# The pooling stage of an odd mixer, interleaved with the gate half of the projection before it

## The chip, the core and the metric

The kernel runs on one core of a Trainium2 chip. The metric is the time of one execution in microseconds (us); a run's time is a little more than the span between its first and last profiled instruction.

## The reference

The program computes two two-layer blocks over 256 tokens of width 2048. The change touches the odd layer of the second block, which is the last layer of the program. In short:

```python
h = u @ w_in_o                                  # 2048 -> 4096
xp, gate = split(h, 2)                          # 2048 columns each
for g, w in enumerate((2, 4, 8, 16)):           # groups of 512 columns
    z[g] = window_mean(xp[g], w, axis=rows) - xp[g]      # over a 4 x 64 grid of tokens
    z[g] = z[g] @ w_pool[g]                     # 512 x 512
y = (concat(z) * pool_scale * silu(gate)) @ w_out_o      # 2048 -> 2048
x = layer_norm(alpha * x + gt * y) * ln_g + ln_b
```

`gt` is a row computed from the conditioning vector (adaptive modulation); the modulation also scales and shifts `x` into `u`.

## The kernel before

**Weights come as a stream.** Every weight is a sequence of slots of 128 x 1024 f32 (512 KB): one slot holds two blocks of 128 rows by 512 columns. The SyncE queue loads slot n into `stage` (a ring of 4, `RING`) as soon as slot n-4 has been split. ScalarE (ACT) writes the high half `wh` (`split_hi`, L257), VectorE (DVE) the rest `wl` (`split_lo`, L278); both are rings of 4 (`SPLITS`), so `split_hi` of slot n waits until TensorE (PE) is done with slot n-4. For a slot PE does 12 matmuls of 128x512 (two row blocks, two token tiles, three products: L325 to L327) and counts it in `split_free`. Eight slots make a group of 512 output columns, accumulated in one of two PSUM tiles `L[0]`, `L[1]`; a group may begin when the group two before it has been evacuated (`psum_free`).

**The stationary operand** is the transposed activation, `xth` and `xtl` (high part and rest). PE transposes two tiles of 128 columns for both token tiles (4 transposes, L404) into one of two PSUM banks `TP`; ACT copies to `xth` (`turn_plain`, L424), DVE subtracts to `xtl` (L430) and frees the bank. The m-th such turn serves the m-th slot of a group.

**The order of the odd layer.** All engines run programs in a fixed order and meet at semaphores:

1. Projection, 8 groups (`R_ODD0`): the first four give `Z` (the pooled half, arena columns 0 to 4095), the last four `gate` (4096 to 8191). ACT evacuates each by Copy (L784). The first group also holds the turns of its input. DVE does one multiply-add of the next modulation (`mod_some`, L569) after every second split. On PE the first two groups are written out and groups 2 to 7 are a loop of three passes, `pe.Fori`, over two groups each.
2. After the last group ACT applies Silu to the whole gate (L1004), and PE computes the sums over tokens, one group of 512 columns after another: 4 plain f32 matmuls (8 passes in the trace, L1975) into the two banks `AB`; DVE scales by the counts and subtracts (L1516), and counts `pooled`. The sums of group g wait for `pooled` of group g-1, since they use the same banks.
3. The pooled `Z` is turned, and the pool product (`R_POOL0`, 8 slots, two for each group) runs between the turns. DVE evacuates group g (`evac_pool`): times `pool_scale` out of PSUM (L1525), then times the gate (L1528).
4. When the last group is through (`y_done`), PE turns the result for the output product (`R_OUTO0`, 4 groups) and ACT issues three loads of 1 MB each, `row_load` (L958): the bias row of the modulation over the gate's columns, `ln_g` and `ln_b` over the windows, the pool scale and what lies beside them. After the first of these groups PE broadcasts the modulation (`modulation_gate`, L1781, 8 passes) and DVE adds the bias row (`gate_rows`, L1456). DVE evacuates each group into the residual. Layer norm and the store of the output follow.

Of the kernel before, what the change touches and what calls it, by code (L numbers as in the profile page):

```python
# [19 lines left out]
P = 128  # L20
# [94 lines left out]
def build(nc, A, out):  # L115
    ctx = ExitStack()
    with ctx:
# [482 lines left out]
        def _(act):  # L600
# [386 lines left out]

            def turn_y(m):
                turn_plain(m)
                if m == 4:  # L990
                    act.wait_ge(once("y_done"), 1)
                    row_load(0, "ln_g", 12288)
# [8 lines left out]
            split_pairs(act, split_hi, R_ODD0, 2, evac_to(0, 1024, 2048), turn=lambda m: turn_modulated(m, 2))  # L1001
            split_pairs(act, split_hi, R_ODD0 + 4, 2, evac_to(4096, 1024, 2048))
            act.wait_ge(psum_free, G_BLOCK1 + R_KV + R_EVEN + R_OUT + R_ODD + 2)
            nc.scalar.activation(ar(4096, 4096), ar(4096, 4096), ACT.Silu).then_inc(once("gate_silu"), 1)  # L1004
            turn_and_split(act, split_hi, R_POOL0, turn_plain)
            act.wait_ge(once("y_done"), 2)
# [3 lines left out]
            split_pairs(act, split_hi, R_OUTO0, R_OUT // 2, None, final=True, turn=turn_plain)  # L1010
# [4 lines left out]
        def _(dve):  # L1015
# [493 lines left out]
            split_pairs(dve, split_lo, R_ODD0, 2, None, turn=turn_x1, beside=lambda i, n: mod_some(64 + 8 * i, n))  # L1509
            split_pairs(dve, split_lo, R_ODD0 + 4, 2, None, beside=lambda i, n: mod_some(80 + 8 * i, n))  # L1510
            Z, gate = ar(0, TT, D), ar(4096, TT, D)
            for g in range(4):
# [7 lines left out]
            def evac_pool(g):  # L1520

                dve.wait_ge(split_free, SPLITS + 8 * R_POOL0 + 2 * g + 2)
                cs = slice(COLS * g, COLS * g + COLS)
                for t in range(TT):
                    ins = nc.vector.tensor_tensor(Z[:, t, cs], L[g % 2][:, t, :], ar(10240 + COLS * g, COLS), ALU.mult)  # L1525
                ins.then_inc(psum_free, 1)
                dve.wait_ge(psum_free, G_BLOCK1 + R_KV + R_EVEN + R_OUT + R_ODD + g + 3)
                ins = nc.vector.tensor_tensor(Z[:, :, cs], Z[:, :, cs], gate[:, :, cs], ALU.mult)  # L1528
                if g == 3:
                    ins.then_inc(once("y_done"), 1)  # L1530

            def turn_z(m):
                turn_plain(m)
                if m == 2:
                    dve.wait_ge(once("pool_row"), 16)
                    dve.wait_ge(once("gate_silu"), 3)
                if m >= 5 and m % 2:
                    evac_pool((m - 5) // 2)

# [3 lines left out]
            def turn_y1(m):  # L1543
                turn_plain(m)
                if m == SLOTS + 1:
                    gate_rows(1)
# [554 lines left out]
```

## Time and profile before

| quantity | value |
|---|---|
| median of three runs | 1954.29 us (1950.17, 1954.29, 1955.58) |
| the profiled execution's own time | 1952.87 us |
| its span, first to last instruction | 1951.0 us |
| PE busy | 1770.0 us, 91% |
| DVE busy | 1331.8 us, 68% |
| ACT busy | 939.3 us, 48% |
| mean granted TensorE clock | 0.957 of full |

Times inside the profile are counted from the span's start. PE is the engine's matmuls, PEld its loads of stationary operands, which overlap them. A matmul's recorded duration overlaps its neighbours', so rates are read from starts, from counts over a stretch, or from the chain, which gives each instruction only the time until the next.

### The profile page before, as it was taken

To read this page: it belongs to the slowest core of one execution; us is meant where nothing else is said; L and a number is where in the kernel's file an instruction comes from. 1 tells how busy PE (TensorE), PEld (TensorE's weight loads), DVE (VectorE), ACT (ScalarE), POOL (GpSimd) and SP (SyncE) were. 2 spreads that over 40 slices of the span, in tenths; PEclk is the share of its full clock that TensorE was granted. 3 is DMA by queue.
4 is the path that set the end of the run, shared out by engine and by line. 5 is a ranking of instruction groups with operands and counts; after the bars stand their busy time and mean duration, and the time that the engine had idled before them with its cause. 6 is when DMAs were issued, how large, how long until landed. Compare 5 with 4: busy or idle time off the path is not lost.

```text
span 1951.0 us, 22381 instructions
## 1 busy us (share of the span) xinstructions
PE 1770.0 (91%) x8116; PEld 1417.6 (73%) x8116; DVE 1331.8 (68%) x1777; ACT 939.3 (48%) x1389; POOL 139.2 (7%) x197
## 2 busy tenths in 40 slices
PE   6998999979998999789999999989998959998894
PEld 5877777868876777568757877777777848885673
DVE  4966777878675777767736677777775556664654
ACT  5445563435365643444464455555533374443334
POOL 0100000111100000111101100000100001110000
PEclk9999999989999999889989999999998979999997
DMA  8855444678654545969936843333846548882551
GB/s 270 288 180 175 150 159 157 206 263 282 225 172 130 176 145 186 317 219 361 315 103 221 281 153 118 113 103 103 316 156 237 192 139 281 289 291 101 186 180 66
DMA packets 107011, 390.30 MB, mean 200 GB/s; under 512 B 12407, under 2 KB 13183, under 8 KB 105215
## 3 DMA queue, kind: packets, MB, share of 16 engines
q1 hardware_dynamic: 75040, 268.99, 39.7%
q0 software_dynamic: 27648, 100.68, 16.8%
q10 hardware_dynamic: 4224, 19.31, 2.6%
q8 instruction: 62, 1.02, 0.2%
q14 instruction: 37, 0.30, 0.0%
HBM read 384.74 MB, written 4.19 MB: 199 GB/s over the span
## 4 chain that ended last, share of the span: by engine, by line
PE 73%; DVE 14%; ACT 5%; DMA 4%; issue 4%; ACTq 0%; SPq 0%; DVEq 0%
PE L L325 20%; PE L L327 19%; PE L L326 19%; DMA mstage<-in_w_mod 3%; PE TP L404 3%; DVE wl L278 3%; DVE macc L569 2%; PE AB L1642 1%; DMA stage<-in_w_stream 1%; PE AB L1571 1%; ACT wh L257 1%; PE AB L1647 1%; PE AB L1975 1%; PE TP L1656 1%; PE AB L1646 1%
## 5 line engine op out<-in xcount | busy, mean ns | idle before, releaser
L278 DVE TENSOR_TENSOR wl<-stage,wh 128x1024 fp32r<-128x1024 f32 x504 | 613.4, 1220 | 321.0 <-ACT wh L257 320.4
L325 PE MATMUL L<-wh,xth 128*128 128x512 f32 x1952 | 797.3, 408 | 7.6 <-DVE wl L278 5.9
L257 ACT ACTIVATE wh<-stage 128x1024 fp32r<-128x1024 f32 x504 | 530.6, 1056 | 498.6 <-PE L L327 417.1
L327 PE MATMUL L<-wh,xtl 128*128 128x512 f32 x1952 | 770.6, 395 | 0.0
L326 PE MATMUL L<-wl,xth 128*128 128x512 f32 x1952 | 769.6, 394 | 0.0
L325 PEld LDWEIGHTS L<-wh,xth 128*128 128x128 f32 x1952 | 373.3, 191 | 101.5 <-issue 19.2
L327 PEld LDWEIGHTS L<-wh,xtl 128*128 128x128 f32 x1952 | 371.6, 190 | 81.4
L326 PEld LDWEIGHTS L<-wl,xth 128*128 128x128 f32 x1952 | 372.6, 191 | 75.4 <-issue 3.4
L569 DVE SCALAR_TENSOR_TENSOR macc<-mstage,scols,macc 128x1024 f32<-128x1024 f32 x240 | 306.7, 1278 | 19.5 <-DMA mstage<-in_w_mod 18.8
L593 POOL DMA_DIRECT2D mstage<-in_w_mod x192 | 138.8, 723 | 1613.2 <-DVE macc L569 1252.2
L879 ACT ACTIVATE arena<-arena 128x256 f32<-128x256 f32 (+1 forms) x136 | 48.2, 426 | 63.6 <-DVE arena L1390 63.5
L1097 DVE SCALAR_TENSOR_TENSOR pa<-tab,AB 128x384 f32<-128x384 f32 x48 | 26.6, 553 | 73.4 <-PE AB L1642 43.4
L679 ACT ACTIVATE pa<-TP 128x384 f32<-128x384 f32 x48 | 23.6, 491 | 108.0 <-PE TP L1656 108.0
L404 PE MATMUL TP<-ident,arena 128*128 128x128 f32 x344 | 55.1, 295 | 22.0 <-DVE xtl L430 7.6
L667 ACT ACTIVATE pa<-pa,st 128x128 f32<-128x128 f32 x96 | 43.0, 448 | 59.8 <-DVE st L1106 36.3
L404 PEld LDWEIGHTS TP<-ident,arena 128*128 128x128 f32 x344 | 44.3, 153 | 33.3 <-issue 9.1
L1571 PE MATMUL AB<-ones,macc 128*128 128x1 f32 x192 | 27.7, 277 | 38.2 <-DVE macc L569 38.2
L404 PE MATMUL TP<-ident,X 128*128 128x128 f32 x144 | 24.5, 302 | 39.5 <-DVE X L1491 19.2
L1571 PEld LDWEIGHTS AB<-ones,macc 128*128 128x128 f32 x192 | 27.9, 231 | 39.8 <-DVE macc L569 39.5
L404 PEld LDWEIGHTS TP<-ident,X 128*128 128x128 f32 x144 | 19.8, 157 | 44.0 <-issue 21.2
L424 ACT ACTIVATE xth<-TP 128x512 fp32r<-128x512 f32 x40 | 23.4, 590 | 52.3 <-PE TP L404 52.3
L643 ACT ACTIVATE arena<-L,st 128x512 f32<-128x512 f32 x60 | 37.8, 682 | 16.8 <-PE L L327 15.4
(184 smaller groups left out, 1391.2 us busy)
## 6 DMA issues: line engine op xcount, KB each, us to landing
stage<-in_w_stream SPq DMA_DIRECT2D x504, 512.0 KB, 4.4
mstage<-in_w_mod POOLq DMA_DIRECT2D x192, 512.0 KB, 6.2
X<-in_x SPq DMA_DIRECT2D x4, 512.0 KB, 8.7
arena<-in_ctx ACTq DMA_DIRECT2D x1, 2048.0 KB, 13.7
x_kept<-X ACTq DMA_DIRECT2D x1, 2048.0 KB, 9.8
X<-x_kept ACTq DMA_DIRECT2D x1, 2048.0 KB, 8.5
arena<-in_b_ada ACTq DMA_DIRECT2D x2, 1024.0 KB, 8.7
arena<-in_ln_b ACTq DMA_DIRECT2D x2, 1024.0 KB, 12.1
```

The costliest lines, as they stand in the source:

```text
L257: nc.scalar.activation(wh[:, s % SPLITS].rearrange("p a b -> p (a b)"), stage[:, s % RING, :], ACT.Copy).then_inc(hi_ready, 1)
L278: nc.vector.tensor_tensor(wl[:, s % SPLITS].rearrange("p a b -> p (a b)"), stage[:, s % RING, :], wh[:, s % SPLITS].rearrange("p a b -> p ...
L325: nc.tensor.matmul(o, xh, w[0], start=start, stop=False, skip_group_check=True)
L326: nc.tensor.matmul(o, xh, w[1], start=False, stop=False, skip_group_check=True)
L327: last = nc.tensor.matmul(o, xl, w[0], start=False, stop=True, skip_group_check=True)
L404: last = nc.tensor.transpose(bank[0:width, j, t * P:t * P + P], src(t), ident[:])
L569: nc.vector.scalar_tensor_tensor(out=acc, in0=block, scalar=col, in1=acc, op0=ALU.mult, op1=ALU.add).then_inc(mod_sum, 1)
L593: pool.dma_start(mstage[:, unit % MOD_UNITS, :].rearrange("p (c n) -> p c n", c=2), WM[n // KPB, :, 2 * cp:2 * cp + 2, COLS * k:COLS * k + ...
L643: ins = nc.scalar.activation(dst(t), L[bank][:, t, :], fn, scale=scale(t))
L667: ins = nc.scalar.activation(pr[b][:, a:a + w], pr[b][:, a:a + w], ACT.Exp, bias=ngm[:, 2 * b + t:2 * b + t + 1], scale=1.0 if swa else ML ...
L879: return nc.scalar.activation(dst, src, ACT.Exp, scale=1.0 / 16)
L1571: last = nc.tensor.matmul(AB[1][:, 384 + 8 * w + j:385 + 8 * w + j], macc[:, w, P * j:P * j + P], ones[:, 0:1], start=True, stop=True)
```

## The change

The odd layer's steps 1 to 4 are put in another order on ACT, DVE and PE; the arithmetic is the same but for the Silu, which now reads the gate's groups from PSUM. The loads on the SyncE and GpSimd queues are as before. The last seven groups of the projection are written out on PE, with no loop.

- The sums of groups 0 to 3 go between slots of the gate groups: after slots 33, 41, 49 and 53 of the projection's 64 (counted from 0). DVE does its part (`pooled`) after its split of slots 38, 46, 54 and 58.
- ACT evacuates the gate groups with Silu (eight pieces of 128x512) in place of Copy and the one large Silu.
- The eight turns of the pooled `Z` follow the eight slots of the last gate group, one each.
- The pool product's eight slots run without those turns. The turns of the result go in pairs (`turn_y`): after pool slots 3, 5 and 7, and before the third slot of the output product. Each pair waits for one group's `y_done` in place of one wait for all.
- `row_load` waits for the fourth `y_done` and comes behind the eighth turn on ACT. `gate_rows` stands after the split of the 11th slot of the output product (the 12th is split after the first residual group).

```diff
+            Z, gate = ar(0, TT, D), ar(4096, TT, D)
             act.wait_ge(mod_cols, MOD_COLS)
             act.dma_start(ar(8192, 3, 512), A["windows"]).then_inc(once("windows"), 16)
             act.dma_start(ar(10240, D), A["pool_scale"][0, :].partition_broadcast(P)).then_inc(once("pool_row"), 16)
-            split_pairs(act, split_hi, R_ODD0, 2, evac_to(0, 1024, 2048), turn=lambda m: turn_modulated(m, 2))
-            split_pairs(act, split_hi, R_ODD0 + 4, 2, evac_to(4096, 1024, 2048))
-            act.wait_ge(psum_free, G_BLOCK1 + R_KV + R_EVEN + R_OUT + R_ODD + 2)
-            nc.scalar.activation(ar(4096, 4096), ar(4096, 4096), ACT.Silu).then_inc(once("gate_silu"), 1)
-            turn_and_split(act, split_hi, R_POOL0, turn_plain)
-            act.wait_ge(once("y_done"), 2)
+            hi.n = 8 * R_ODD0 + 4
+            ODD, POOL, OUTO = 8 * R_ODD0, 8 * R_POOL0, 8 * R_OUTO0
+            for m in range(2):
+                turn_modulated(m, 2)
+            for n in range(4, 68):
+                if n < 10:
+                    turn_modulated(n - 2, 2)
+                hi()
+                if n >= 60:
+                    turn_plain(n - 60)
+                if n % 8 == 3 and n > 8:
+                    g = (n - 11) // 8
+                    slots_done(act, ODD + n - 3)
+                    for t in range(TT):
+                        dst = (Z if g < 4 else gate)[:, t, COLS * (g % 4):COLS * (g % 4) + COLS]
+                        ins = nc.scalar.activation(dst, L[g % 2][:, t, :], ACT.Copy if g < 4 else ACT.Silu)
+                    ins.then_inc(psum_free, 1)
+            hi(4)
+            for i in range(4):
+                if i:
+                    hi(2)
+                for m in range(2 * i, 2 * i + 2):
+                    turn_plain(m)
+            act.wait_ge(once("y_done"), 5)
             row_load(1, "b_ada", 4096)
             row_load(1, "ln_g", 12288)
             row_load(1, "ln_b", 8192)
-            split_pairs(act, split_hi, R_OUTO0, R_OUT // 2, None, final=True, turn=turn_plain)
+            hi(OUTO + 4 * SLOTS - hi.n)
             layer_norm_act(1, 2 * DEPTH + 3)
...
-            split_pairs(dve, split_lo, R_ODD0, 2, None, turn=turn_x1, beside=lambda i, n: mod_some(64 + 8 * i, n))
-            split_pairs(dve, split_lo, R_ODD0 + 4, 2, None, beside=lambda i, n: mod_some(80 + 8 * i, n))
+            lo.n = 8 * R_ODD0 + 4
             Z, gate = ar(0, TT, D), ar(4096, TT, D)
-            for g in range(4):
+            GO = G_BLOCK1 + R_KV + R_EVEN + R_OUT
+            def pooled(g):
                 dve.wait_ge(once("pool_sums"), g + 1)
                 for t in range(TT):
                     z = Z[:, t, COLS * g:COLS * g + COLS]
...
             def evac_pool(g):
-                dve.wait_ge(split_free, SPLITS + 8 * R_POOL0 + 2 * g + 2)
+                slots_done(dve, 8 * R_POOL0 + 2 * g + 2)
                 cs = slice(COLS * g, COLS * g + COLS)
+                if g == 0:
+                    dve.wait_ge(once("pool_row"), 16)
+                    dve.wait_ge(psum_free, GO + R_ODD + 2)
                 for t in range(TT):
                     ins = nc.vector.tensor_tensor(Z[:, t, cs], L[g % 2][:, t, :], ar(10240 + COLS * g, COLS), ALU.mult)
                 ins.then_inc(psum_free, 1)
-                dve.wait_ge(psum_free, G_BLOCK1 + R_KV + R_EVEN + R_OUT + R_ODD + g + 3)
-                ins = nc.vector.tensor_tensor(Z[:, :, cs], Z[:, :, cs], gate[:, :, cs], ALU.mult)
-                if g == 3:
-                    ins.then_inc(once("y_done"), 1)
-            def turn_z(m):
-                turn_plain(m)
-                if m == 2:
-                    dve.wait_ge(once("pool_row"), 16)
-                    dve.wait_ge(once("gate_silu"), 3)
-                if m >= 5 and m % 2:
-                    evac_pool((m - 5) // 2)
-            turn_and_split(dve, split_lo, R_POOL0, turn_z)
-            evac_pool(3)
-            def turn_y1(m):
-                turn_plain(m)
-                if m == SLOTS + 1:
-                    gate_rows(1)
-            split_pairs(dve, split_lo, R_OUTO0, R_OUT // 2, evac_residual(1), final=True, turn=turn_y1)
+                dve.wait_ge(psum_free, GO + R_ODD + g + 3)
+                nc.vector.tensor_tensor(Z[:, :, cs], Z[:, :, cs], gate[:, :, cs], ALU.mult).then_inc(once("y_done"), 1)
+            for m in range(2):
+                turn_x1(m)
+            for n in range(4, 68):
+                if n < 10:
+                    turn_x1(n - 2)
+                lo()
+                mod_some(64, n - 4)
+                if n in (38, 46, 54, 58):
+                    pooled((38, 46, 54, 58).index(n))
+                if n >= 60:
+                    turn_plain(n - 60)
+            lo(2)
+            evac_pool(0)
+            lo(2)
+            evac_pool(1)
+            for i in range(4):
+                if i:
+                    lo(2)
+                if i in (1, 2):
+                    evac_pool(i + 1)
+                for m in range(2 * i, 2 * i + 2):
+                    turn_plain(m)
+            lo(5)
+            gate_rows(1)
+            evac_o = evac_residual(1)
+            for g in range(4):
+                if g:
+                    lo(min(8, 8 * R_OUTO0 + 4 * SLOTS - lo.n))
+                slots_done(dve, 8 * R_OUTO0 + 8 * g + 8)
+                evac_o(g // 2, g % 2)
...
             G = G_BLOCK1 + R_KV + R_EVEN + R_OUT
-            product_pairs(pe, R_ODD0, G, 4, turn=xt_group(pe, u, X, R_ODD0, G,
-                                                          lambda m: pe.wait_ge(once("ln_done"), m // 2 + 1)))
-            pe.wait_ge(psum_free, G + R_ODD + 2)
-            pe.wait_ge(once("windows"), 16)
             WIN, Z = ar(8192, 3, TT, TOK), ar(0, TT, D)
-            for g in range(4):
-                if g:
+            def pool_sums(g):
+                pe.wait_ge(psum_free, G + g + 1 + 2)
+                if g == 0:
+                    pe.wait_ge(once("windows"), 16)
+                else:
                     pe.wait_ge(once("pooled"), g)
                 for t in range(TT):
                     for j in range(TT):
...
                                                 Z[:, j, COLS * g:COLS * g + COLS], start=j == 0, stop=j == 1)
                 last.then_inc(once("pool_sums"), 1)
-            def pool_step(m):
-                g = m // 2
-                if m % 2 == 0:
-                    pe.wait_ge(psum_free, G + R_ODD + g + 1)
-                pe.wait_ge(lo_ready, 8 * R_POOL0 + m + 1)
-                for k in range(KPB):
-                    last = products(L[g % 2], m % SPLITS, k, KPB * m + k, m % 2 == 0 and k == 0)
-                last.then_inc(split_free, 1)
-            xt_pe(pe, u, Z, pool_step, lambda m: pe.wait_ge(once("pooled"), m // 2 + 1))
-            pe.wait_ge(once("y_done"), 2)
-            product_pairs(pe, R_OUTO0, G + R_ODD + 4, 2, turn=xt_group(pe, u, Z, R_OUTO0, G + R_ODD + 4),
-                          after=lambda: modulation_gate(1))
+            def turn_z(m):
+                transposes(pe, u, [lambda t, kt=2 * m + j: Z[:, t, kt * P:kt * P + P] for j in range(2)])
+                return u.n
+            xt_group(pe, u, X, R_ODD0, G, lambda m: pe.wait_ge(once("ln_done"), m // 2 + 1))()
+            uses = []
+            for n in range(SLOTS, 8 * SLOTS):
+                g, m = n // SLOTS, n % SLOTS
+                slot(pe, 8 * R_ODD0 + n, G + g, KPB * m, m == 0)
+                if n in (33, 41, 49, 53):
+                    pool_sums((33, 41, 49, 53).index(n))
+                if g == 7:
+                    pe.wait_ge(once("pooled"), m // 2 + 1)
+                    uses.append(turn_z(m))
+            ys = []
+            def turn_y(i):
+                pe.wait_ge(once("y_done"), i + 2)
+                for m in range(2 * i, 2 * i + 2):
+                    ys.append(turn_z(m))
+            for m in range(SLOTS):
+                turned(pe, uses[m])
+                slot(pe, 8 * R_POOL0 + m, G + R_ODD + m // 2, KPB * m, m % 2 == 0)
+                if m in (3, 5, 7):
+                    turn_y((m - 3) // 2)
+            for n in range(4 * SLOTS):
+                g, m = n // SLOTS, n % SLOTS
+                if n == 2:
+                    turn_y(3)
+                if g == 0:
+                    turned(pe, ys[m])
+                slot(pe, 8 * R_OUTO0 + n, G + R_ODD + 4 + g, KPB * m, m == 0)
+                if n == 7:
+                    modulation_gate(1)
```

## Rows read from the trace of the kernel before

**Rows 1.** Top of the page: the span.
```profile
span 1951.0 us, 22381 instructions
...
```

**Rows 2.** Stretches: PE, PEld, DVE, ACT, POOL busy (instructions), clock, DMA share, GB/s.
```profile
...
1637.00:1767.30 130.30, 130.30 (x576) 107.62 (x574) 86.69 (x73) 56.62 (x60) 15.91 (x22) 1.00 0.85 285
1767.36:1854.74 87.38, 71.09 (x289) 50.99 (x290) 45.48 (x53) 31.16 (x36) 0.00 (x0) 0.94 0.38 133
1829.40:1923.40 94.00, 94.00 (x413) 75.96 (x411) 47.97 (x50) 32.72 (x34) 0.00 (x0) 0.99 0.46 156
...
```

**Rows 3.** Chain of work that ended last, 1764 to 1833: start, us, what.
```profile
...
1767.12 0.24 PE L L327
...
1769.52 5.41 PE AB L1975 x8
1774.96 1.42 DVE arena L1516 x2
1776.42 3.71 PE AB L1975 x8
...
1796.11 0.44 PE TP L404 x4
...
1799.32 0.44 PE TP L404 x4
...
1816.87 0.24 PE L L327
1817.19 1.07 ACT wh L257
1818.29 1.23 DVE wl L278
...
1820.74 1.23 DVE arena L1528
...
1829.43 0.43 PE L L325
...
```

**Rows 4.** The same chain, 1590 to 1870, where it meets line L1781.
```profile
...
1854.74 3.70 PE AB L1781 x8
...
```

**Rows 5.** Line L257, the high halves, 1637 to 1767.3: idle before it, times.
```profile
...
  PE L L327: 73.8, 48
...
```

**Rows 6.** Groups by line, 1590 to 1767: busy us, mean ns, idle before.
```profile
...
L278 DVE TENSOR_TENSOR wl<-stage,wh 128x1024 fp32r<-128x1024 f32 x63 | 77.2, 1225 | 56.3 <-ACT wh L257 56.3
...
L569 DVE SCALAR_TENSOR_TENSOR macc<-mstage,scols,macc 128x1024 f32<-128x1024 f32 x30 | 38.3, 1277 | 0.0
...
L784 ACT ACTIVATE arena<-L 128x512 f32<-128x512 f32 x14 | 7.5, 582 | 0.0
...
L430 DVE TENSOR_TENSOR xtl<-pa,xth 128x512 fp32r<-128x512 f32 x6 | 4.1, 684 | 0.0
...
```

**Rows 7.** Timeline of ACT, 1755 to 1860: start, us, instruction.
```profile
...
1769.48 1.28 ACT L1004 ACT_TABLE_LOAD   x1
1770.78 3.62 ACT L1004 ACTIVATE arena<-arena 128x4096 f32<-128x4096 f32 x1
1791.00 1.08 ACT L424 ACTIVATE xth<-TP 128x512 fp32r<-128x512 f32 x2 [16.61 <-PE TP L404]
...
1826.44 0.45 ACTq L958 DMA_DIRECT2D arena<-in_ln_b  x1
...
```

**Rows 8.** Transfers issued from 1820 to 1860: size, median us to landing.
```profile
...
arena<-in_ln_b ACTq DMA_DIRECT2D x1, 1024.0 KB, 9.8
```

**Rows 9.** Line L958, the row loads, in the whole span.
```profile
...
DMA to landing us min/median/max: 5.5/8.7/14.5
```

**Rows 10.** Instruction transfers, 1829.4 to 1923: packets, MB, share.
```profile
...
q8 instruction: 4, 0.07, 0.3%
...
```

**Rows 11.** The same from 1590 to 1767, and the stream of slots there.
```profile
...
q8 instruction: 3, 0.05, 0.1%
...
stage<-in_w_stream SPq DMA_DIRECT2D x62, 512.0 KB, 4.8
...
```

## Prediction

> **What bounds the kernel now.** I read the span [rows 1], then a table of stretches [rows 2], then the chain of work that ended last [rows 3]. From 1637 to 1767.3 PE is never idle at the full clock of 2.4 GHz: 576 matmuls, exactly six groups, in 130.3 us, so a slot of 12 costs 2.715 us. The product after the pooling stage, 1829.4 to 1923.4, is as dense. Between them lies the changed stage. From the end of the projection (1767.12 + 0.24 = 1767.36) to the start of the modulation's broadcast at 1854.74 [rows 3, 4] it takes 87.38 us, with PE busy for 71.09 of them, part of that at a lower clock (mean 0.94) [rows 2]. The reader should see four kinds of loss in the chain:
>
> - Before the first sums ACT must evacuate: 1767.36 to 1769.52.
> - Between two groups' sums DVE works alone, 1.42 us for its two instructions, where PE needs 3.71 for eight passes. The first sums, after idle time, take 5.41.
> - From 1817.11 to the first matmul of the output product at 1829.43 the chain is mostly ACT and DVE: split, scale, gate, two groups in turn, then a turn.
> - That product starts with matmuls of 0.43 us, the level of 1.2 GHz; dense matmuls follow each other in 130.3 / 576 = 0.226.
>
> So PE bounds its neighbours and dependences bound this stage. What is taken off it comes off the end, provided PE's stream stays fed.
>
> **The sum.** I count what PE must do between the same two points once the order is changed, and then ask whether anything makes it wait.
>
> - Sums: 4 x 3.70 = 14.8 us, now between slots. Their nearest row under such conditions is the broadcast, also eight f32 passes with slots on both sides: 3.70 [rows 4]; the isolated sums say 3.71 [rows 3]. Bounds 3.70 and 5.41 each; the latter needs the lower clock, which PE shows only after idle time, so I take 3.70.
> - A slot with its turn takes 1799.32 - 1796.11 = 3.21 us [rows 3], so a turn costs 3.21 - 2.715 = 0.495. Eight turns in the last gate group: 3.96. Eight for the result: 3.96.
> - Pool product, eight slots: 21.72. First group of the output product: 21.72.
>
> Together 66.2 us. Before it is 87.4, so 21.2 us go. The span becomes 1929.8, the profiled execution's time 1952.87 - 21.2 = 1931.7. That execution lies 1.4 below the median of the runs shown; from the median, 1954.29 - 21.2 = 1933.1. I predict 1933.
>
> **What hides the rest, with its margin.** Let E be the end of the projection's last slot in the new order; PE's program gives pool slots 1, 3, 5 and 7 ending at E + 5.9, 11.4, 17.8 and 24.2, and the broadcast at E + 47.9.
>
> *DVE in the gate half.* For two slots it has two splits of 1.225 and one multiply-add of 1.277: 3.7 of 5.43 us [rows 6]. Each `pooled` adds 1.42, while PE spends 3.70 more on the sums it belongs to. In the last group two slots last 6.42 and hold two more subtractions of 0.68: 5.1. Each `pooled` is placed after a split which itself needs a slot that PE runs after the sums, so DVE does not wait there; and the next sums come seven slots later. For the last pair it is three slots, 8.1 us, against split, split, multiply-add and `pooled`, 5.0. Behind the DVE wait stand the splits, on which PE has three slots of lead. I cost it at nothing; without cover it is 4 x 1.42 = 5.7 us.
>
> *ACT.* It idled 73.8 us before 48 splits, 1.54 each [rows 5]. A large Silu (3.62 for 4096 columns, 0.45 for 512) and a Copy from PSUM (0.58 for 512) [rows 6, 7] bound the new Silu piece: 0.45 to 1.03, if both costs added. I take 0.58: the same eviction in another function. After the last slot ACT has a split (1.07), a turn (0.58) and two pieces: the bank is free at about E + 3, or E + 4, and PE wants it at E + 5.9. Also nothing.
>
> *The four pairs of result turns* are new waits of PE, and behind them stand the pool slots. Each needs: split high, split low, scale, gate. The trace has this very chain: PE's slot ends at 1817.11, the gate product at 1820.74 + 1.23 = 1821.97, 4.86 us later [rows 3]. PE comes for the first pair two slots after the one that releases the chain, 5.43 us: 0.57 to spare. For the other three a pair of turns lies between, 6.42 us: 1.56 to spare. The turn banks must be free too; DVE's subtractions follow the gate product by two times 0.68, and PE returns to a bank 5.4 us later. Nothing, but thin.
>
> *The row loads.* They issued at 1826, 28 us ahead of the broadcast. Now they come behind the eighth turn on ACT, at about E + 33 to E + 34. The last landed 9.8 us after its issue [rows 7, 8], so at E + 44; the longest landing of such a load is 14.5 [rows 9], E + 48.7. DVE asks for them at E + 47.4. The margin is 3.4 us by the first row and -1.3 by the second. Queued behind DVE are the 12th split and the first residual evacuation; PE would wait for the banks in its third broadcast.
>
> *The stream of slots.* A load is released by the split four slots earlier and must land before the split of its slot, four slots of PE less the two splits, 10.9 - 2.3 = 8.6 us; slots land in 4.8 us in the busy half [rows 11]. The modulation's transfers keep their order; the pauses of PE relieve both.
>
> **One rule of the skill, against rows.** Silu now stands between Copies on ACT. The row shows one table load of 1.28 us ahead of Silu and none ahead of the Copy that follows at 1791.00 [rows 7]; I count one load, as before. If each of the four gate evacuations switched there and back, then at the last group, by this row's 1.3 us, split, turn, load, two pieces and load end at E + 5.4, and the first result would be ready at about E + 11.4, just when PE wants it: 0 to 0.5 us lost. The Trainium skill (ScalarE: Activation LUTs, What ACT_TABLE_LOAD costs) puts a switch at 2.66 us with its drain and advises to finish one set's calls before another's. By its figure that result would come at E + 14, an estimate, and the time would be near 1936. The same page says that Copy is in every set; by that the trace agrees.
>
> **Rivals.**
>
> 1. *Late results.* One of the thin margins is missed, at each pair of turns or at the rows. If the 4.86 becomes 7 us (another ACT split in front, a later slot), the pairs lose 1.6 + 3 x 0.6 = 3.4 us; rows 14.5 us late add 1.3; a short spell at 0.43 per matmul after such a wait adds about 1.2 (six matmuls at 0.2 more). Time 1934 to 1940. For it speaks the 0.57; against it, that ACT and DVE are both idle when each chain begins.
> 2. *Reloads of the table at each switch*: worked out above from the row, 1933 to 1934.
> 3. *Instruction supply, the slower side.* The loop's 576 matmuls are replaced by written-out code while the DMA share is 0.85. The output product, written out, took 4 instruction packets for 413 recorded matmuls; 576 need 5.6, where 3 were fetched over the whole projection [rows 2, 10, 11]. If each fetch stalled PE, the gain is gone at 21.2 / 5.6 = 3.8 us a packet, the result is slower by over 0.3% at (21.2 + 5.9) / 5.6 = 4.8, and at the landing of a slot there, 4.8 us [rows 11], it is 1933 + 27 = 1960. Against it: written-out code runs without a gap at 0.99 clock in the output product [rows 2]. The Trainium skill (Runtime: NRT & Kernel Launch, Instruction fetch mechanics) says that straight code is fetched ahead, mostly hidden, and that a taken branch breaks this; by that the loop's removal could only gain, but the dense loop shows nothing to be gained.
> 4. *The change does not do what it says*: `pooled` or the sums wait and the pooled tiles come late, so that the stage stays serial. Then most of 21.2 us stays, 1948 to 1957. The placement above speaks against it.
>
> **Chances.** 0.3% is 5.9 us, about what a measurement of this kernel can tell from no change. The forecast has 0.74 (1929 to 1936: runs here differ by up to 5.4 us, and their median by some 3), late results 0.15, reloads 0.03, instruction supply 0.05 (0.01 faster, 0.01 within, 0.03 slower), no overlap 0.03 (0.02 within 0.3%, 0.01 faster). Faster 0.94, same 0.03, slower 0.03. The range runs from 1929 to 1940, the upper end being rival 1 with all its terms; what is left out is rivals 3 and 4 and the edges, under 0.2.
>
> **What would show it.** In the profile of the changed kernel: L1975's idle time before it near zero and each eight passes in 3.7 us; PE without a pause over 0.5 us from 1594 to the end of the output product; the clock at 1.00 in that stretch, with no matmuls of 0.43 in it; the first broadcast pass near 1833.5; one table load in the gate half. The prediction is wrong if PE waits ahead of the pairs of turns for L1528, if DVE waits for the rows ahead of L1456, or if written-out slots of the projection take longer than 2.72 us.

## The result

| | before | changed |
|---|---|---|
| median of the runs | 1952.23 us (1950.0 to 1955.58, 4 runs) | 1932.79 us (1927.22 to 1934.9, 4 runs) |
| span of the profiled execution | 1951.0 us | 1930.4 us |

The ratio of the changed kernel to the one before is 0.9897, 95% interval 0.9873 to 0.9921: faster, by 1.0%. In a second measurement (run 9) it was 0.9893 (0.9874 to 0.9911). The forecast was 1933.0, with 1929 to 1940 around it.

Executions differ by some microseconds ahead of the changed stage, so the comparisons below use the **stage time**: from the start of the odd projection's first matmul to the start of the modulation's first broadcast pass, both read from PE's timeline. What comes behind is the **tail**.

| | first matmul | broadcast | stage | tail |
|---|---|---|---|---|
| before | 1588.66 | 1854.58 | 265.92 | 96.42 |
| changed | 1590.71 | 1833.98 | 243.27 | 96.42 |
| changed, second execution | 1587.59 | 1830.60 | 243.01 | 96.40 |

The stage gave 22.65 us. The spans differ by 20.6 because the changed kernel's profiled execution reached the projection 2.05 us later. That part of the program is the same in both, and the second execution reached it 3.1 earlier than the first; it is no effect of the change. The two executions of the changed kernel also differ inside the stage, by 0.26 us, and all of it lies ahead of the last turn of the gate group: from there to the broadcast both take 47.63 us (1786.35 to 1833.98, and 1782.97 to 1830.60). Where a run is judged by a few tenths, this **last part** is used.

### The profile page after: what moved, and what is told of

It is laid out like the page before. It is cut to its first block, busy times and chain, and to the rows that moved or that the text cites. A ratio compares the mean times of both kernels' runs of the same rounds, so it can differ in the third digit from the quotient of the medians.

```text
span 1930.4 us, 22331 instructions
## 1 busy us (share of the span) xinstructions
PE 1765.5 (91%) x8116; PEld 1416.2 (73%) x8116; DVE 1331.3 (69%) x1777; ACT 935.3 (48%) x1388; POOL 139.3 (7%) x197
## 3 DMA queue, kind: packets, MB, share of 16 engines
q8 instruction: 65, 1.06, 0.2%
## 4 chain that ended last, share of the span: by engine, by line
PE 74%; DVE 13%; ACT 6%; DMA 4%; issue 3%; SPq 0%; ACTq 0%; DVEq 0%
PE L L325 20%; PE L L327 20%; PE L L326 20%; PE TP L404 3%; DVE wl L278 2%; DMA mstage<-in_w_mod 2%; DVE macc L569 2%; PE AB L1678 1%; PE AB L1607 1%; DMA stage<-in_w_stream 1%; ACT wh L257 1%; PE AB L1683 1%; PE TP L1692 1%; PE AB L1682 1%; PE AB L1969 1%
## 5 line engine op out<-in xcount | busy, mean ns | idle before, releaser
L257 ACT ACTIVATE wh<-stage 128x1024 fp32r<-128x1024 f32 x504 | 530.6, 1056 | 505.5 <-PE L L327 437.6
L419 ACT ACTIVATE pa<-TP,gcols 128x256 f32<-128x256 f32 x42 | 17.4, 463 | 54.4 <-PE TP L404 54.4
```

Source lines behind the costliest of these rows:

```text
L257: nc.scalar.activation(wh[:, s % SPLITS].rearrange("p a b -> p (a b)"), stage[:, s % RING, :], ACT.Copy).then_inc(hi_ready, 1)
```

## The profile after

The table of stretches of the changed kernel (busy time of PE, PEld, DVE, ACT, POOL with the number of instructions; granted clock, DMA share, GB/s). The first row runs from the end of the slow start of the projection to the broadcast, the second is a part of what the second row of [rows 2] covers: the four pairs of turns with the eight slots between and behind them, from the end of pool slot 3 on:

```profile
...
1594.90:1833.90 239.00, 239.00 (x1067) 192.80 (x1066) 162.94 (x154) 108.31 (x127) 20.96 (x29) 1.00 0.74 248
1797.88:1823.00 25.12, 25.12 (x128) 21.15 (x127) 22.14 (x26) 12.37 (x16) 0.00 (x0) 1.00 0.54 194
...
```

PE has no idle time in 239 us and the clock is 1.00 throughout. In the second row DVE is busy 22.14 of 25.12 us, a number that matters below.

Line L2012 (the sums, L1975 before) in the same kernel, with what its engine waited for ahead of it:

```profile
...
L2012 PE MATMUL AB<-arena x32: 590/592/593, 1687.6 to 1755.3; 128*128 128x512 f32 x32
...
  issue: 5.8, 24
...
```

Thirty-two passes as before, none of 1057 ns any more as in the slow first group, and no wait for DVE. The 5.8 us of "issue" stand for weight loads, which overlap the passes. PE's timeline around the first of the four groups shows the price:

```profile
...
1687.34 0.39 PE L327 MATMUL L<-wh,xtl 128*128 128x512 f32 x1
1687.56 3.59 PE L2012 MATMUL AB<-arena 128*128 128x512 f32 x8
...
1691.22 0.40 PE L326 MATMUL L<-wl,xth 128*128 128x512 f32 x1
...
```

The slot's last matmul starts at 1687.34 and the second of the next at 1691.22. Two dense matmuls account for 0.45 of the 3.88, so eight passes cost 3.43, not the 3.70 of [rows 4] or 3.71 of [rows 3]. The broadcast's row holds a short wait for DVE ahead of its third part. The isolated sums have nothing behind them, and their 3.71 counts the last pass to its recorded end, 0.59 after its start.

ACT in the gate half, timeline (start, us):

```profile
...
1708.67 1.28 ACT L1018 ACT_TABLE_LOAD   x1
1709.96 1.09 ACT L1018 ACTIVATE arena<-L 128x512 f32<-128x512 f32 x2
1710.93 1.06 ACT L257 ACTIVATE wh<-stage 128x1024 fp32r<-128x1024 f32 x1
...
1733.76 1.06 ACT L1018 ACTIVATE arena<-L 128x512 f32<-128x512 f32 x2
...
```

One table load, ahead of the first Silu piece, and none before the Copy (L257) or at the next gate evacuation (1733.76). A Silu piece lasts as long as the Copy before: two in 1.06 to 1.09.

The first result on DVE (the gating, L1553), and the next slot's end as ACT sees it (the split at 1797.96 starts when pool slot 3 has ended):

```profile
...
1796.07 1.23 DVE L1553 TENSOR_TENSOR arena<-arena 128x1024 f32<-128x1024 f32 x1
...
```

```profile
...
1797.96 1.06 ACT L257 ACTIVATE wh<-stage 128x1024 fp32r<-128x1024 f32 x1 [1.66 <-PE L L327]
...
```

The result is there at 1796.07 + 1.23 = 1797.30; PE asks for it when slot 3 ends, 0.08 ahead of the split, at 1797.88. That leaves 0.58 us, where 0.57 was forecast. But a matmul's recorded end lies behind the start of the next, and PE's turns start earlier than 1797.88:

```profile
...
1797.70 1.03 PE L404 MATMUL TP<-ident,arena 128*128 128x128 f32 x8
...
1804.04 1.04 PE L404 MATMUL TP<-ident,arena 128*128 128x128 f32 x8
...
1810.40 1.03 PE L404 MATMUL TP<-ident,arena 128*128 128x128 f32 x8
...
1816.73 1.04 PE L404 MATMUL TP<-ident,arena 128*128 128x128 f32 x8
...
```

So 0.40 us was really left (runs 5 and 11 give 0.47 and 0.38). These four rows also give PE's period of two slots and a pair of turns, 6.33 to 6.36 us. The wait for the rows, transfers issued between 1815 and 1835:

```profile
...
arena<-in_ln_b ACTq DMA_DIRECT2D x1, 1024.0 KB, 11.8
```

The third load was issued at 1818.66 and landed at 1830.5; DVE's last split before the bias row ended at 1832.61 + 1.23. So 3.4 us were left, as forecast. DVE then still waited until 1835.10 for the broadcast's first passes, so by these rows a landing up to 4.6 us later would not have shown.

## Experiments

Twelve kernels ran beside the pair. Four build the change up part by part (1 to 4), four press on its margins (5 to 8), one repeats the changed kernel (9), two are faster versions (10 and 12), and one looks into a missed expectation (11). Runs 5 to 8 and 11 were executed once each.

### 1. Only the loop written out

```diff
-            product_pairs(pe, R_ODD0, G, 4, turn=xt_group(pe, u, X, R_ODD0, G, ...))
+            xt_group(pe, u, X, R_ODD0, G, ...)()
+            for n in range(SLOTS, 8 * SLOTS):
+                slot(pe, 8 * R_ODD0 + n, G + n // SLOTS, KPB * (n % SLOTS), n % SLOTS == 0)
```

> The kernel before, with only the projection's last seven groups written out on PE in place of the loop. The measure is the stage time, from the first matmul of the odd projection to the first pass of the modulation's broadcast: 265.6 us before (1589.0 to 1854.6), 242.9 with the whole change. Dependence theory (the gain is the closing of waits between engines): 265.6, no change in the run's time. Rival, instruction supply: written-out code costs, up to 5.6 packets at 3.8 us or more, 287 us. Second rival, the loop itself was costing something and its removal is part of the gain: under 265.

Ratio 1.0001 (0.9986 to 1.0015); stage 265.65 us against 265.92, a difference like that between two executions of one kernel. Written-out code fetches more, and waits for nothing. Instruction transfers of this kernel from 1620 to 1750, then PE from 1632 to 1761:

```profile
...
q8 instruction: 5, 0.08, 0.2%
...
```

```profile
...
1632.00:1761.00 129.00, 129.00 (x571) 106.82 (x570) 85.42 (x72) 56.05 (x60) 15.91 (x22) 1.00 0.85 285
...
```

Five packets, against three over the whole projection before [rows 11], and 571 recorded matmuls in 129.0 us, 0.226 each as in [rows 2], at a DMA share of 0.85. The slower rival is out, and the loop had cost nothing either. The Trainium skill (Runtime: NRT & Kernel Launch, Instruction fetch mechanics) says that a block crossing is mostly hidden; by that the trace agrees.

### 2. The sums between slots, and nothing else

As 1, with `pool_sums` after slots 33, 41, 49, 53 on PE and `pooled` after splits 38, 46, 54, 58 on DVE, as in the change. Silu whole, turns of the pooled tiles in the pool product, one wait for the result.

> As the run before this one, and the sums over tokens are placed between slots of the gate groups, with the vector engine's part beside its splits; Silu whole and late, the turns and the waits on results as in the kernel before. The isolated sums took 26.0 us from the last projection matmul to the first pool matmul. Dependence theory: PE now spends 13.7 on the sums inside the projection, but after it ACT still does a split (1.07), two evacuations (0.98), a table load (1.28) and the whole Silu (3.62) before the first turn, so the first pool matmul comes some 8.5 us after the last slot: stage 265.6 - 26.0 + 13.7 + 8.5 = 261.8, a gain of only 4. Rival (each part adds its own share, and the sums' four waits and slow start are most of it): a gain of 10 or more, 255.

Ratio 1.0003 (0.9988 to 1.0017); stage 265.16. The move gained 0.5 us against run 1 and 0.8 against the kernel before, not 4. The chain of work that ended last, from the projection's end in this kernel:

```profile
...
1779.77 1.06 ACT wh L257
...
1781.82 1.28 ACT L1004
1783.11 3.62 ACT arena L1004
...
1788.08 1.09 PE TP L404 x4
1789.17 0.43 PE L L325
...
```

The first pool matmul comes 9.5 us after the last slot (1779.69), not 8.5; part of the difference is the turn, which takes 1.09. And PE had idled while ACT did its Silu, so the turn and the first eight matmuls run at 1.2 GHz, 0.43 us a matmul in place of 0.23: 1.6 us. (The granted clock was 0.55 of full from 1788 to 1793.) The kernel before had kept PE at work on the sums in that time and began the pool product at full clock. The expectation left the clock out: 26.0 - 13.7 - 9.5 - 1.6 = 1.2. Another 0.5 goes at the start of the output product, where eight matmuls are slow in this run and six were before.

### 3. And Silu in pieces

```diff
-            nc.scalar.activation(ar(4096, 4096), ar(4096, 4096), ACT.Silu)...
+                        ins = nc.scalar.activation(dst, L[g % 2][:, t, :], ACT.Copy if g < 4 else ACT.Silu)
```

> As the run before this one, and the gate groups are evacuated with Silu in pieces. Dependence theory: 4.9 us of ACT (table load and whole Silu) leave the path ahead of the first turn, so the stage is 257, 5 less than the run before. Rival (Silu was beside the path, as in the kernel before, where it ran under the sums): no difference, 262.

Ratio 0.9957 (0.9943 to 0.9971); stage 258.17, 7.0 less than 2. The same place of the chain:

```profile
...
1775.77 0.97 ACT arena L1014 x2
1776.74 0.50 ACT xth L424
...
1778.10 0.63 PE TP L404 x4
...
```

Table load and Silu (4.9 us) are gone between evacuation and turn, and the third turn takes 0.63 in place of 1.09: after this shorter spell, 3.5 us from the last slot with two turns in it, the granted clock was still 1.00, which gives the other 2. In the kernel before, Silu ran under the first sums [rows 3, 7]; it had become the price of moving them.

### 4. All but the pairs of result turns

The changed kernel, with PE's result turns behind one wait for the fourth `y_done`, and ACT and DVE in the order of the kernel before from the pool product on:

```diff
-                if m in (3, 5, 7):
-                    turn_y((m - 3) // 2)
+            pe.wait_ge(once("y_done"), 5)
+            product_pairs(pe, R_OUTO0, G + R_ODD + 4, 2, turn=xt_group(pe, u, Z, R_OUTO0, G + R_ODD + 4),
+                          after=lambda: modulation_gate(1))
```

> The changed kernel, with its result turns put back: all eight after the last group's result, the splits and evacuations in the order of the kernel before. Sums, Silu in pieces and the turns of the pooled tiles in the last gate group stay. Dependence theory: the end of the pool product shows the old gap of 12.3 us (1817.1 to 1829.4 before) and six matmuls at half the clock (1.3), less the 1.0 of the first two turns: stage 242.9 + 12.6 = 255.5. So the pairs of turns are over half of the gain of 22.6. Rival (the sums are most of it): under 248.

Ratio 0.9942 (0.9927 to 0.9957); stage 255.64 against 255.5 expected. The chain shows what the pairs remove:

```profile
...
1809.20 1.07 ACT wh L257
1810.30 1.23 DVE wl L278
1811.53 1.21 DVE arena L1545 x2
1812.76 1.23 DVE arena L1548
...
1815.12 1.21 DVE arena L1545 x2
1816.35 1.24 DVE arena L1548
...
1820.33 1.12 PE TP L404 x4
1821.45 0.43 PE L L325
...
```

So the steps, in this order, are worth: loop 0.3, sums 0.5, Silu pieces 7.0, the turns of the pooled tiles in the last gate group 2.5, pairs of result turns 12.4 to 12.6. The sum is 22.65 by construction; the shares belong to this order. Silu in pieces without moving the sums was not run; that it would have gained little is argued from its place under the first sums.

### 5 and 6. More DVE work ahead of each result

```diff
                 ins.then_inc(psum_free, 1)
+                for e in range(k):      # k = 1, then 3
+                    link(nc.vector.tensor_tensor(ar(12288, 1024), ar(10240, 1024), ar(11264, 1024), ALU.mult))
                 dve.wait_ge(psum_free, GO + R_ODD + g + 3)
```

> The changed kernel with one more DVE instruction of 128x1024 (a product of two constant rows into unused space, followed by a wait for its end; about 1.25 us) between the scaling and the gating of each pooled group. Margin theory: the first pair of turns has 0.57 us to spare and the other three 1.56, so PE loses 0.7 us once and nothing after: stage 242.9 + 0.7 = 243.6. Rival (DVE is the bound of the pool product): 4 x 1.25 = 5 us, 247.9.

> The same with three such instructions, about 3.8 us for each group. Margin theory: the first pair is 3.2 late; the others each 3.8 - 1.56 = 2.2 late if DVE has caught up in between, and a delay of PE by the first pair also delays the slots that release the next: stage 242.9 + 3.2 + 3 x 2.2 = 252.7, PE waiting ahead of each pair for the gating. DVE as a bound without margins: 4 x 3.8 = 15, 258. Hidden: 243.

Stages 246.00 and 257.39, so 2.7 and 14.1 us lost, where 0.7 and 9.8 were expected; by the last part, 2.5 and 14.2. The second lies beside the forecast of the rival, DVE as the bound (258). DVE's timeline with one extra instruction (L1553 is it; L1550 is the scaling, L1555 the gating):

```profile
...
1803.22 1.23 DVE L1555 TENSOR_TENSOR arena<-arena 128x1024 f32<-128x1024 f32 x1
1804.37 1.28 DVE L430 TENSOR_TENSOR xtl<-TP,xth 128x512 fp32r<-128x512 f32 x2
1805.56 2.35 DVE L278 TENSOR_TENSOR wl<-stage,wh 128x1024 fp32r<-128x1024 f32 x2
1807.83 1.28 DVE L1550 TENSOR_TENSOR arena<-L,arena 128x512 f32<-128x512 f32 x2
1809.03 1.21 DVE L1553 TENSOR_TENSOR arena<-arena 128x1024 f32<-128x1024 f32 x1
1810.28 1.23 DVE L1555 TENSOR_TENSOR arena<-arena 128x1024 f32<-128x1024 f32 x1
...
```

There is no idle time in these rows, and from one gating to the next it is 7.06 us (1803.22 to 1810.28). PE's own work for two slots and two turns is 6.36. DVE's work without the extra instruction is 7.06 - 1.25 = 5.8, so it had 0.6 us free in each period, not 1.56. On PE the first pair starts 12.13 us after the last turn of the gate group, where the changed kernel has 11.35: 0.78 later for 1.25 more work, a margin of 0.47. The next three pairs follow after 6.56, 7.05 and 7.06 us, so the full period cost 0.7 at each of the last two. The 1.56 was the spare time of one chain, and a chain's spare time says nothing about whether the engine can do so much in every period. With three instructions the period is 9.57 (1804.99 to 1814.56 in that run), 3.2 over. PE waits 10.1 us in all, and the rest of the loss is slow clock behind the waits: the granted clock was 0.66 of full from 1805 to 1810 and 0.70 from 1825 to 1830.

### 7. The table switched at each gate evacuation

```diff
                     ins.then_inc(psum_free, 1)
+                    if g >= 4:
+                        nc.scalar.activation(arena[:, 12288 + g:12289 + g], ident[:, 0:1], ACT.Sqrt)
```

> The changed kernel with one Sqrt of a single column after the evacuation of each gate group, so that ACT must load its tables twice for each (eight loads in place of one). By the row of 1.28 us a load: at the last group ACT is later by a load ahead of Silu, a load and a small instruction behind it (2.8 us), which just uses up what it has before pool slot 4: the first result comes about 0 to 0.5 us late, stage 243 to 243.5. By the figure of the Trainium skill (ScalarE: Activation LUTs, What ACT_TABLE_LOAD costs) of 2.66 a switch, an estimate of 2.6 us late, 245.5.

Stage 243.71, 0.4 to 0.7 us over the changed kernel. PE's timeline shows where: the third turn of the last gate group starts 3.45 us after the second in place of 3.20, behind the switches of the third group, and the first pair of result turns 11.57 after the last of those turns in place of 11.35. ACT at the last gate group:

```profile
...
1785.70 1.28 ACT L1018 ACT_TABLE_LOAD   x1
1787.00 1.09 ACT L1018 ACTIVATE arena<-L 128x512 f32<-128x512 f32 x2
1788.10 1.28 ACT L1021 ACT_TABLE_LOAD   x1
1789.40 0.20 ACT L1021 ACTIVATE arena<-ident 128x1 f32<-128x1 f32 x1
...
```

A load takes 1.28 and the next instruction starts 0.02 later. The Trainium skill (ScalarE: Activation LUTs, What ACT_TABLE_LOAD costs) has 2.66 us a switch with its drain; no such drain stands in these rows, and the measured stage fits 1.3. The tail was 95.32, 1.1 less: the last Sqrt had left the table for the layer norm's root in place, and no load stands ahead of that root in this trace.

### 8. The row loads four slots later

```diff
+            hi(4)
             row_load(1, "b_ada", 4096)
```

> The changed kernel with the three row loads issued four slots of the output product later on ACT, some 10 to 11 us. Margin theory: in the changed kernel the last of them landed 3.4 us before DVE asks for the rows, so now DVE waits about 7 us ahead of the bias row; PE waits in its third broadcast, about 7 us less the 1.5 us that the broadcast has in hand, and the span grows by 5 to 7. Rival (the slots that are already split hide it): no change of the span.

The stage did not change (243.52), the tail grew by 9.0 us, to 105.40. DVE's first bias row, and PE's two halves of the broadcast:

```profile
...
1844.11 1.29 DVE L1477 TENSOR_TENSOR arena<-AB,arena 128x512 f32<-128x512 f32 x2 [7.65 <-DMA arena<-in_ln_b]
...
```

```profile
...
1836.60 1.88 PE L1818 MATMUL AB<-macc,ones 128*128 128x512 f32 x4
1844.86 3.78 PE L1818 MATMUL AB<-macc,ones 128*128 128x512 f32 x4 [6.38 <-DVE arena L1477]
...
```

DVE waited 7.65 us for the third load (about 7 expected), and PE 6.38 ahead of its third broadcast (5.5 expected). The passes behind the wait took 3.78 for four in place of 1.88, and matmuls of 0.43 followed: this is 1.2 GHz again, and the 2.6 us above the 6.4 are its price. The expectation, 5 to 7 in all, had left it out.

### 9. The changed kernel once more

> The changed kernel once more, on the same chip as the next run, as its reference: ratio to the kernel before 0.990, stage 242.9 us.

Ratio 0.9893 (0.9874 to 0.9911), stage 243.01.

### 10. The sums as fp32r products

PE bounds the whole stretch, so taking its work away should come off the end. The pooled input is split like every other operand and the windows, which are zeros and ones, are copied to fp32r once; `zl` is a new tile, made room for by letting `scols` share the tile `ccols`, and the rest lies in the tiles of the first block's latents.

```diff
+                    nc.scalar.activation(zh, Z[:, :, COLS * q:COLS * q + COLS], ACT.Copy).then_inc(once("zh"), 1)
...
+                    nc.vector.tensor_tensor(zl[:, :, :], Z[:, :, COLS * q:COLS * q + COLS], zh.bitcast(F32),
+                                            ALU.subtract).then_inc(once("zl"), 1)
...
-                        last = nc.tensor.matmul(AB[t][:, :], WIN[...], Z[...], start=j == 0, stop=j == 1)
+                        nc.tensor.matmul(AB[t][:, :], w, zh[:, j, :], start=j == 0, stop=False, skip_group_check=True)
+                        last = nc.tensor.matmul(AB[t][:, :], w, zl[:, j, :], start=False, stop=j == 1, skip_group_check=True)
```

> The changed kernel with the sums over tokens as two fp32r products each (the pooled input split into a high part by ACT and a rest by DVE; the window matrices are zeros and ones, so the sum stays as exact as the other products). PE does 8 matmuls of 0.227 us for each group (1.8) where it did 8 passes in 3.43. If PE's own work is now the bound of the whole stretch, as the theory says, 4 x 1.6 = 6.5 us come off the end: stage 236.4, ratio to the kernel before near 0.986. If DVE or ACT, which get 1.22 and 1.06 us more for each group, or the stream of slots has become the bound, nothing comes off: 242.9.

Ratio 0.9858 (0.9838 to 0.9878) beside 0.9893 for the changed kernel on the same chip, with medians of 1924.41 and 1929.71 us; stage 236.77, 6.2 to 6.5 less. The first group's sums on PE's timeline, from the first product to the next slot:

```profile
...
1688.41 0.39 PE L2035 MATMUL AB<-lxh,lxl 128*128 128x512 f32 x1
...
1690.24 0.39 PE L331 MATMUL L<-wh,xth 128*128 128x512 f32 x1
...
```

1.83 us a group in place of 3.43. The 4 x 1.6 us came off entirely, and DVE's and ACT's extra work did not show: PE has no wait in the stretch, and the last part is 47.63 us again.

### 11. More ACT time in the chains, no more DVE

Between the slot's end and the split that starts each of the four result chains, ACT gets a Copy of 128x1024. (The note in brackets in the expectation is wrong: all four chains have it.)

```diff
+            def late_hi(n):
+                slots_done(act, n - 3)
+                link(nc.scalar.activation(ar(12288, 1024), ar(10240, 1024), ACT.Copy))
+                hi()
```

> The changed kernel with one more ACT instruction (a Copy of 128x1024 into unused space and a wait for its end, about 1.1 us) between the end of the slot that starts each of the first four result chains (pool slots 1, 3, 5, 7) and the split that the chain begins with. One more DVE instruction of 1.25 us in the same chain cost the stage 2.7 us, where margins of 0.57 and three times 1.56 had said 0.7. Theory now: a chain may grow within its margin, but DVE has only 0.6 us of free time in each 6.4 us of the pool product, and an extra 1.25 us of DVE work overruns that. So 1.1 us of ACT in the same chain costs only what the first margin lacks: stage 243.2 + 0.5 = 243.7. Rival (the margins themselves were over-counted, the chain's length costs): as before, about 2.5 us, stage 245.5 or more. (The fourth chain's split is left as it is where it comes after the third pair: three of the chains in fact get the extra instruction behind a slot's end that ACT waits for, and the fourth through the slot before.)

Stage 244.62: 1.4 to 1.6 us lost, between the two; by the last part, 1.4. PE's four pairs of turns:

```profile
...
1794.77 1.09 PE L404 MATMUL TP<-ident,arena 128*128 128x128 f32 x8 [0.52 <-DVE arena L1567]
...
1801.18 1.03 PE L404 MATMUL TP<-ident,arena 128*128 128x128 f32 x8
...
1807.99 1.16 PE L404 MATMUL TP<-ident,arena 128*128 128x128 f32 x8 [0.33 <-DVE xtl L430]
...
1814.48 1.03 PE L404 MATMUL TP<-ident,arena 128*128 128x128 f32 x8
...
```

The first pair waits for its result, with 0.52 us of recorded idle time, but it starts 12.06 us after the last turn of the gate group, 0.71 later than in the changed kernel: of 1.09 us more in the chain, 0.38 was covered. The third does not wait for its result but for a turn bank: DVE's subtraction for the pair before (L430). That subtraction comes behind the gating, so a bank is free 0.68 us later than the result, the second 1.28 later. In the changed kernel it ends at 1810.27 for the second tile of the second pair, and PE wants that bank at about 1811.0: 0.75 to spare, not 1.56. So of the miss in 5, the larger part is DVE's full period (0.7 at each of the last two pairs), and the chains' true margin was about half of what was forecast. Here the first pair lost 0.8 us and the third 0.6, counted to the start of the pair behind each; the second and the fourth lost nothing.

### 12. And the tables of the layer norms loaded early

```diff
+                if m == 9:
+                    nc.scalar.activation(nmu[:, 0:1], ident[:, 0:1], ACT.Sqrt)
...
             row_load(1, "ln_b", 8192)
+            nc.scalar.activation(nmu[:, 1:2], ident[:, 0:1], ACT.Sqrt)
```

> The kernel with the fp32r sums, and a Sqrt of one column on ACT ahead of each of the two layer norms of the second block, at a place where ACT is idle, so that the table for Sqrt is loaded beside the products. Each of the two loads of 1.28 us lies on the path now (between the squares and the root). Theory: the stage stays at 236.8, the tail from the broadcast to the end goes from 96.4 to 95.1, and as much again comes off ahead of the stage: 2.6 us less than the fp32r kernel, ratio to the kernel before near 0.984 to 0.985. Rival (the load was beside other work): no difference.

Ratio 0.9845 (0.9827 to 0.9863), median 1922.84 us, the fastest version. Its interval overlaps that of run 10, and it ran on another chip, so the measured times do not tell the two apart; the trace does: tail 95.34 in place of 96.43, and no table load ahead of the root of either layer norm. The stage was 237.19, 0.4 over run 10, all of it ahead of the last gate turn; the last part is 47.64. The load now lies on ACT beside the product:

```profile
...
1807.80 1.28 ACT L1048 ACT_TABLE_LOAD   x1 [0.16 <-issue]
1809.09 0.20 ACT L1048 ACTIVATE st<-ident 128x1 f32<-128x1 f32 x1
...
```

## Why the prediction was right, step by step

- *What bounds it*: right. Stage by stage the loss was waits between engines, and with them closed PE is busy in all 239 us. Run 10 shows the other half of the statement: 6.4 us of PE's work taken away came off in full.
- *The sum*: 66.2 us forecast for the new order between the projection's last matmul and the broadcast, 21.2 saved; 22.65 measured on the stage. The term that was mis-sized is the sums, 4 x 3.70 where 4 x 3.43 were needed: 1.1 of the 1.45. The nearest row that the prediction took, the broadcast, held a wait for DVE. Another 0.3 is the turns in pairs: 6.34 less two slots of 2.715 is 0.91 for two, not 0.99. The hit on the median is closer than the reasoning was, by luck: 21.2 was taken off 1954.29, while the result's medians, 1952.23 and 1932.79, lie 19.4 apart and those of run 9 21.9.
- *DVE and ACT in the gate half*: costed at nothing, and PE waited for neither.
- *The four pairs*: costed at nothing, and they cost nothing. The first margin was 0.58 against 0.57 by the count to slot 3's recorded end, but 0.40 to PE's start, and runs 5 and 11 give 0.47 and 0.38. The other three were said to be 1.56; run 11 and the free time of DVE in run 5 put them at about 0.75 for the bank and 0.6 for the period. The prediction let PE return to a turn bank 5.4 us after DVE's subtraction; in DVE's order that subtraction comes behind the next gating, and PE returns 0.75 us after it. A conclusion that held on wrong numbers.
- *The row loads*: 3.4 us to spare, as forecast, by two errors that cancel. With E at 1786.51 the third load was issued at E + 32.1, not up to E + 34, and took 11.8 us to land, not 9.8. Run 8 shows what stood behind it.
- *The table*: one load, as forecast; at eight loads 0.4 to 0.7 us, by the trace's row of 1.28 a load and not by the 2.66 of the Trainium skill (ScalarE: Activation LUTs, What ACT_TABLE_LOAD costs).
- *Instruction supply*: shown to cost nothing (run 1). *No overlap*: not seen.

One thing the prediction left unsaid: its sum counts PE's work in the finished order, so it is good for the whole change and says nothing of a part. The sums alone were worth 0.5 us; in the order run here, the gain came only with Silu cut up behind them.

## What to carry to other kernels

When waits between engines are closed by reordering, count for each new meeting point two things: the spare time of its chain, up to the last resource that comes free (here the turn bank, not the result), and the load of each engine in one period of the new order. And look at what ran under the wait that is removed, because it comes out from under it: here a table load and Silu of 4.9 us, which then stopped PE long enough to halve its clock.

## What the runs showed of the hardware

- Eight plain f32 passes between dense fp32r matmuls cost 3.43 us, 0.43 each; two rows of the same kind in the kernel before said 3.70 and 3.71, the one with a wait for DVE in it, the other with nothing behind the last pass. As two fp32r products each, the same sums took 1.83 us (run 10).
- A wait of PE has a second price, the slow spell behind it. After 8.4 us from the last slot to the next turn, with two turns in them, that turn and the matmuls behind it took 2.1 us more (run 2: 0.5 and 1.6), after 6.38 us without work some 2.6 (run 8); after 3.5 us, with two turns in them, none (run 3).
- A table load on ACT was 1.28 us with the next instruction 0.02 us behind it; run 7 has eight of them and lost 0.4 to 0.7 us in all. With the table for the root loaded at an idle place, the tail was 1.1 us shorter (run 12).
